# A two-block model step on one core: three weight pieces taken together at the start of each stage, their halves made ahead of the norm

## The reference

```python
mod = silu(c) @ w_ada + b_ada                 # shifts, scales, gates ("ada")
h = rms_norm(x, w) * (1 + sc1) + sh1
x = x + g1 * mixer(h)                         # gated delta rule; GLA; MLA
h = rms_norm(x, w) * (1 + sc2) + sh2
x = x + g2 * (silu(gu[:, :D_FF]) * gu[:, D_FF:]) @ w_out   # gu = h @ w_in
```

## Time and profile before

| | us |
|---|---|
| median of 3 runs | 1551.38 |
| lowest and highest | 1547.1, 1552.73 |
| profiled execution, its own time | 1547.16 |
| its span in the profile | 1545.6 |
| mean granted TensorE clock in it | 0.958 of 2.4 GHz |

### The profile page before, as it was taken

The page is one execution under the profiler, slowest core; times in us unless marked ns, Lnnn a source line. Parts: engine busy times, 40 slices in busy tenths (PEclk is TensorE's granted clock), DMA queues, the critical chain, the costliest instruction groups (busy, mean ns, idle before and its releaser), DMA issues.

```text
span 1545.6 us, 27829 instructions
## 1 busy us (share of the span) xinstructions
PE 1433.0 (93%) x10169; PEld 1261.8 (82%) x10169; DVE 747.8 (48%) x1452; ACT 644.4 (42%) x1171; POOL 14.8 (1%) x81
## 2 busy tenths in 40 slices
PE   5999999999998889999979998899998899899997
PEld 2977888887885678899947777799997678799997
DVE  0666656666532144455456543655553122555553
ACT  3454544445322044445364432555542222555542
POOL 3000000000000000000000000000000000000000
PEclk9899999999998989999979999899999889899999
DMA  8666457564553759965639983466564125266562
GB/s 292 178 206 203 150 151 232 187 196 136 166 148 125 214 151 290 273 183 160 173 109 291 282 271 96 137 185 181 162 180 157 29 86 135 70 185 180 167 187 83
DMA packets 400010, 269.89 MB, mean 175 GB/s; under 512 B 9914, under 2 KB 357424, under 8 KB 399936
## 3 DMA queue, kind: packets, MB, share of 16 engines
q1 hardware_dynamic: 399936, 268.83, 58.6%
HBM read 267.75 MB, written 1.05 MB: 174 GB/s over the span
## 4 chain that ended last, share of the span: by engine, by line
PE 76%; DMA 8%; DVE 7%; ACT 4%; issue 2%; SPq 2%; DVEq 0%; ACTq 0%
PE bank L715 16%; PE bank L716 15%; PE bank L717 15%; PE bank L680 5%; DMA w_raw<-in_w_in 4%; PE bank L758 4%; PE bank L651 3%; PE bank L666 2%; PE bank L1080 1%; DMA big<-in_w_ada 1%; DMA ring<-in_w_gdn_proj 1%; PE bank L888 1%; DVE w_low L1658 1%; PE bank L889 1%; PE bank L1112 1%
## 5 line engine op out<-in xcount | busy, mean ns | idle before, releaser
L715 PE MATMUL bank<-h_parts,w_high 128*128 128x256 f32 x1824 | 550.5, 302 | 17.0 <-DVE h_parts L1674 15.4
L716 PE MATMUL bank<-h_parts,w_high 128*128 128x256 f32 x1824 | 523.1, 287 | 0.0
L717 PE MATMUL bank<-h_parts,w_low 128*128 128x256 f32 x1824 | 522.4, 286 | 0.0
L1658 DVE TENSOR_TENSOR w_low<-w_raw,w_high 128x1024 fp32r<-128x1024 f32 (+2 forms) x324 | 359.5, 1122 | 184.2 <-ACT w_high L1223 184.0
L715 PEld LDWEIGHTS bank<-h_parts,w_high 128*128 128x128 f32 x1824 | 355.7, 195 | 43.8 <-issue 25.3
L716 PEld LDWEIGHTS bank<-h_parts,w_high 128*128 128x128 f32 x1824 | 357.5, 196 | 3.9 <-issue 3.6
L717 PEld LDWEIGHTS bank<-h_parts,w_low 128*128 128x128 f32 x1824 | 356.7, 196 | 0.0
L1223 ACT ACTIVATE w_high<-w_raw 128x1024 fp32r<-128x1024 f32 (+2 forms) x324 | 312.6, 973 | 81.4 <-DMA w_raw<-in_w_in 38.0
L1215 ACT ACTIVATE evac<-bank 128x256 f32<-128x256 f32 x140 | 53.9, 385 | 232.9 <-PE bank L717 183.3
L715 PE MATMUL bank<-act_parts,w_high 128*128 128x256 f32 x528 | 149.3, 283 | 0.0
L717 PE MATMUL bank<-act_parts,w_low 128*128 128x256 f32 x528 | 148.6, 281 | 0.0
(11 more groups left out here) (338 smaller groups left out, 1495.6 us busy)
## 6 DMA issues: line engine op xcount, KB each, us to landing
w_raw<-in_ffn_w_in SPq DMA_DIRECT2D x88, 512.0 KB, 3.8
w_raw<-in_w_in SPq DMA_DIRECT2D x72, 512.0 KB, 4.0
ada_w<-in_ada_w SPq DMA_DIRECT2D x34, 1024.0 KB, 5.4
w_raw<-in_w_ffn_in SPq DMA_DIRECT2D x44, 512.0 KB, 6.4
ada_w<-in_w_ada SPq DMA_DIRECT2D x16, 1024.0 KB, 11.5
w_raw<-in_gla_w_in SPq DMA_DIRECT2D x24, 512.0 KB, 6.4
w_raw<-in_ffn_w_out SPq DMA_DIRECT2D x32, 384.0 KB, 3.8
w_raw<-in_ffn_w_out SPq DMA_DIRECT2D x32, 320.0 KB, 3.0
```

What stands on the lines that cost most here:

```text
L715: pe.matmul(acc[:, 0:T], hi[:, n, :], x_parts[:, k, 0, :], start=k == 0, stop=False)
L716: pe.matmul(acc[:, 0:T], hi[:, n, :], x_parts[:, k, 1, :], start=False, stop=False)
L717: mm = pe.matmul(acc[:, 0:T], lo[:, n, :], x_parts[:, k, 0, :], start=False, stop=k == kb - 1)
L1658: dve.tensor_tensor(w_low[:, s, 0:m], w_raw[:, s, 0:m], w_high[:, s, 0:m].bitcast(F32), ALU.subtract)\
```

## The change

At each opening TensorE takes three pieces (two in the first mixer) together, one block of h after the other: for each block, nine (six) matmuls into three (two) banks. The high and low halves of those pieces are made ahead of the norm: in FFN 1 between the copies of w_o's product, in FFN 2 in the GLA's last head, in FFN 3 before the last heads' attention. The high half of the fourth piece comes directly behind the norm. `high` waits on another condition for first slots. The first round of hidden pieces uses four banks. `st_o2` and `st_o3` move to ring slots that leave `w_raw`, `w_high` and `w_low` free for pieces 0 to 2. In the first mixer the low halves of pieces 0 and 1 move ahead of the norm's scale. Between FFN 1 and the GLA the squares of the second norm go from ScalarE to VectorE, and GLA pieces 1 and 2 get their low halves before the next scaling; two `rows2` steps move. Nothing of SP's code is changed.

```diff
@@ SplitStream
+        self.parts_free = [max(Stream.slot_user.get(self.SLOTS + s, 0), Stream.slot_user.get(2 * self.SLOTS + s, 0)) for s in range(slots)]
@@ program
-        st_o2 = Stream(1, KB, [3, 7, 11, 16, 17, 0, 1, 2])
+        st_o2 = Stream(1, KB, [3, 7, 11, 16, 17, 12, 13, 14])
-        st_o3 = Stream(1, KB, SplitStream.SLOTS)
+        st_o3 = Stream(1, KB, [12, 13, 14, 15, 16, 17, 7, 11])
@@ TensorE, ffn
-                for i in range(6 if ada else 0):
+                pe.wait_ge(S("evacuated"), st_f.block0 + 3)
+                for k in range(KB):
+                    for j in range(3):
+                        split_product(st_f, 0, j, bank[j], h_parts, IN_PARTS[0], KB, ready=("h_low", parts_made) if j == 0 else None, part=[k])
+                split_product(st_f, 0, 3, bank[3], h_parts, IN_PARTS[0], KB)
+                for i in range(1, 6 if ada else 1):
                     hidden(i)
@@ TensorE, head1
-                    some(3 * KB)
+                    for k in range(KB):
+                        for j in range(2):
+                            split_product(st_h1, i, j, bank[j], h1_parts, IN_PARTS[0], KB, part=[k], ready=None if j else ("h_low", 0))
+                    at[0] = 2 * KB
+                    some(KB)
@@ TensorE, head2
-                    products(KB)
+                    for k in range(KB):
+                        for j in range(3):
+                            split_product(st_h2, i, j, bank[j], h1_parts, IN_PARTS[0], KB, part=[k], ready=None if j else ("h_low", LOW_OF[3] * KB))
+                    at[0] = 3 * KB
+                    rows2(2)
                     low_rank()
                     products(KB)
+                    rows2(3)
                     gate_channels()
-                    for step in range(2, 6):
+                    for step in range(4, 6):
@@ ScalarE, high
-                if st is not st_h1 or not (isinstance(i, int) and i == 0 and j < st.slots):
+                if isinstance(i, int) and i == 0 and j < st.slots:
+                    if st in (st_f1, st_f2, st_f3):
+                        act.wait_ge(S("gemm_done"), st.parts_free[j])
+                    elif st is not st_h1:
+                        act.wait_ge(S("gemm_done"), st.block0)
+                else:
                     act.wait_ge(S("gemm_done"), st.done(i, j) - st.slots)
@@ ScalarE, out_blocks
-                        copy_out(st, i, j, evac[:, j, :], 2, scale=mod[:, bass.ds(per * i + gate * KB + j, 1)])
+                        copy_out(st, i, j, evac[:, j, :], 2, scale=mod[:, c:c + 1])
+                        if (per * i + j) % 2 and per * i + j < 6:
+                            high(st_f, 0, (per * i + j) // 2, IN_PARTS)
@@ ScalarE, ffn
-                act.wait_ge(S("gemm_done"), st_f.block0)
-                high(st_f, 0, 0, IN_PARTS)
                 norm(n)
+                high(st_f, 0, 3, IN_PARTS)
                 for f in range(KB):
...
-                    if f % 4 == 3:
-                        high(st_f, 0, f // 4 + 1, IN_PARTS)
@@ ScalarE, between the stages
-            for f in range(KB):
-                act.wait_ge(S("h_ready"), 2 * KB + f + 1)
-                act.activation(sq[:, f, :], xT[:, f, :], ACT.Square).then_inc(S("norm_sq"), 1)
@@ ScalarE, the GLA's last head (behind its second token copy); and behind the MLA's last softmax, for st_f3
+                    for j in range(3):
+                        high(st_f2, 0, j, IN_PARTS)
@@ VectorE, add_blocks
+                        if f % 2 and f < 6:
+                            low(st_f, 0, f // 2, IN_PARTS)
@@ VectorE, ffn
-                low(st_f, 0, 0, IN_PARTS)
...
-                for j in (1, 2):
-                    low(st_f, 0, j, IN_PARTS)
@@ VectorE, between the stages
-            norm_apply(2, xT)
+            for f in range(KB + 1):
+                if f < KB:
+                    dve.scalar_tensor_tensor(xT[:, f, :], xT[:, f, :], nscale[:, f:f + 1], rstd[:, :], ALU.mult, ALU.mult).then_inc(S("h_scaled"), 1)
+                if f:
+                    dve.wait_ge(S("h_ready"), 2 * KB + f)
+                    dve.tensor_tensor(sq[:, f - 1, :], xT[:, f - 1, :], xT[:, f - 1, :], ALU.mult).then_inc(S("norm_sq"), 1)
+            for j in (1, 2):
+                low(st_h2, 0, j, IN_PARTS)
@@ VectorE, the GLA's last head; and behind the MLA's last softmax, for st_f3
+                    for j in range(3):
+                        low(st_f2, 0, j, IN_PARTS)
                     ada_bias(3, 0, 12, len(early) + H1 + st_pa.n + 12)
```

More of the change, by code:

```diff
@@ L731, in hidden @@
                             ada(i, j // 2)
-                for i in range(6 if ada else 0):
+                pe.wait_ge(S("evacuated"), st_f.block0 + 3)
[4 more added lines that the diff above has]
+                for i in range(1, 6 if ada else 1):
                     hidden(i)
-                with pe.Fori(6 if ada else 0, st_f.n) as i:
+                with pe.Fori(6 if ada else 1, st_f.n) as i:
                     hidden(i)
@@ L1421, in hidden @@
                         act.wait_ge(S("ffn_free"), first + 2 * i + j // 2 + 1)
-                        copy_out(st_f, i, j, evac[:, j, :], 2, func=ACT.Silu if j % 2 == 0 else ACT.Copy)
+                        copy_out(st_f, i, j, evac[:, j, :], 4 if isinstance(i, int) and i == 0 else 2, func=ACT.Silu if j % 2 == 0 else ACT.Copy)
                         if j < 1:
-                            high(st_f, i, j + 3, IN_PARTS)
+                            if not (isinstance(i, int) and i == 0):
+                                high(st_f, i, j + 3, IN_PARTS)
                         elif not last:
@@ L1429, in hidden @@
                         if j % 2:
-                            dst = act_parts[:, 2 * i + j // 2, 0, :] if last else act_parts[:, bass.ds(2 * i + j // 2, 1), 0, :]
+                            dst = act_parts[:, 2 * i + j // 2, 0, :] if isinstance(i, int) else act_parts[:, bass.ds(2 * i + j // 2, 1), 0, :]
                             act.wait_ge(S("ffn_act"), first + 2 * i + j // 2 + 1)
                             act.activation(dst, evac[:, j - 1, :], ACT.Copy).then_inc(S("act_high"), 1)
-                with act.Fori(0, st_f.n - 1) as i:
+                hidden(0)
+                with act.Fori(1, st_f.n - 1) as i:
                     hidden(i)
@@ L1534, in head2 @@
                 copies(5)
+                if not gemm:
+                    for j in range(3):
+                        high(st_f2, 0, j, IN_PARTS)
                 act.wait_ge(S("o2_done"), n)
@@ L1627, in _ @@
             softmax(st_h3.n - 1)
+            for j in range(3):
+                high(st_f3, 0, j, IN_PARTS)
             attended(st_h3.n - 1)
@@ L1700, in _ @@
             h_low(0, KB - 1, h1_parts)
-            for j in (1, 2):
-                low(st_h1, 0, j, IN_PARTS)
+            low(st_h1, 0, 2, IN_PARTS)
             dve.wait_ge(S("rows_landed"), 16 * n_table_dmas)
@@ L2006, in ffn @@
                 add_down(st_d, 2 + FFN_OF[n] * KB, batch)
-            add_blocks(st_o1, 4, "o_added", 4)
+            add_blocks(st_o1, 4, "o_added", 4, st_f1)
             def bias_ffn1():
@@ L2023, in _ @@
             h_low(3, KB - 1, h1_parts)
-            for j in (1, 2, 3):
-                low(st_h2, 0, j, IN_PARTS)
+            low(st_h2, 0, 3, IN_PARTS)
             dve.memset(segment, 1.0).then_inc(S("segment"), 1)
@@ L2183, in _ @@
             softmax(st_h3.n - 1)
+            for j in range(3):
+                low(st_f3, 0, j, IN_PARTS)
             add_pairs(st_o3, 4 + 2 * KB)
```

23 lines of the change are left out of this document (12 added, 11 removed).

## The result

The changed kernel takes 1558.39 us (median; 1553.85 to 1562.59) where the kernel before takes 1546.51 us in the same comparison: ratio 1.0074, 95% interval 1.0051 to 1.0098, 11.9 us slower. The profiled execution took 1561.79 us, its span is 1560.3 us and its mean granted clock 0.953, against 1545.6 us and 0.958 before.

The account below looks back on a forecast made before the run. TensorE, three quarters of the chain that ended last, was taken as the bound, mostly its split products. Lost 19.3 us less gained 7.8 made 11.5 us slower; 1551.4 + 11.5 is 1563 us, range 1553 to 1573.

Parts of the forecast that it names:

- The output projection: w_o before FFN 1: ScalarE waits for a piece's landing, TensorE stalls 7.4 us, slow clock 1.5 more; 8.9 us lost.
- From hidden to output: Each FFN: w_out's first high half waits for all hidden products, 2.3 us late; 6.9 us lost, plus 2.2 for clock.
- The last head: GLA's last head: FFN 2's low halves take 3.5 us on VectorE, 2.2 of it idle; 1.3 us lost.
- The FFN openings: First 72 products, interleaved with early halves: gains of 2.0 us in FFN 1, 1.4 in FFN 2, 2.3 in FFN 3.
- The bounds of 3 and 12 us: FFN and first mixer openings together: gain 3 us with 7 us at low clock, 12 with none; 6.8 taken.
- The first mixer's opening: First mixer's first 72 products, two pieces interleaved: 11.3 against 12.4 us, 1.1 us gained.
- The GLA: GLA stage, norms and interleaved opening up to piece 5: 1 us gained, between -1.5 and +2.5.
- the first (cheap waits): Rival for all gaps and openings: waits cost no clock, openings gain 2 us more; 1557 us, chance 0.24.
- The second: Rival in the first mixer's head loop: shifted transfers save 5 us on each of six, 1533 us; chance 0.04.
- The third: Rival at the openings: bank switching every third product keeps TensorE at 1.2 GHz, 24 us more, 1587 us; chance 0.05.

Follow-up runs that it names:

- e6: Changed kernel, but SP issues FFN 1's first three pieces behind the first four blocks of w_o instead of all eight: 1550.61 us, 1.0042 of the kernel before.
- e2: Changed kernel with FFN 1's three early high and low halves made behind the copies of w_o's blocks 5 and 6: 1550.25 us, 1.0018 of the kernel before.
- e1: Changed kernel with the old first-slot wait for all streams but those of the hidden pieces: 1554.31 us, 1.0041 of the kernel before.
- e5: Kernel before with only the wait of the w_out streams' first slots for all hidden products added: 1558.24 us, 1.0090 of the kernel before.
- e4: e3 with FFN 2's three low halves moved behind the state updates of the GLA's last head: 1539.98 us, 0.9945 of the kernel before.
- e9: e8 with the high half of each FFN's fourth piece made ahead of the norm: 1536.81 us, 0.9945 of the kernel before.
- e8: e4 with two instead of three pieces interleaved in the GLA's opening, gate channels one piece earlier: 1537.23 us, 0.9956 of the kernel before.
- e10: The same program as e4, run once more: 1539.70 us, 0.9961 of the kernel before.
- e7: e4, but TensorE takes the FFNs' first three pieces one after another: 1542.16 us, 0.9983 of the kernel before.
- e3: Changed kernel with the edits of e1 and e2 together: 1545.61 us, 0.9983 of the kernel before.
- e11: The same program as e8, run once more beside e10: 1537.01 us, 0.9950 of the kernel before.

## Why the prediction held

1563 us was forecast, 1558.4 measured (11.5 slower forecast, 11.9 measured). The mechanism was the one forecast: two added waits that cost more than the openings gain. That the difference was met to 0.4 us is luck in part: the terms below were off by up to 3 us each, and the errors cancel. The 4.6 us by which the time itself was missed come from the base: 1551.4 was the median of three executions, and that of eight is 1546.5.

- **The output projection** (7.4 us stall, 1.5 clock): 7.66 and 3.1. e6 shows the landing as the cause, e2 that the whole goes away with it. The clock term was too small, as I let only 16 products run slowly and the trace shows 3.1 us over 48; for those 16 my own rows gave 1.7 (5.22 less 3.5), not 1.5.
- **From hidden to output** (2.3 us three times, 0.7 each for the clock): 1.98 to 1.99, and no clock loss in the changed kernel. e1 shows the wait as the cause. With the clock neither end was wrong: e5 lost it behind two gaps of three.
- **The last head** (1.3): 1.1 by the gap, and 1.7 of clock that was not in the sum. e4 takes both away. I had charged a gap that grows only with its growth; behind the longer gap the products ran slowly too (5.41 us instead of 3.72). The other 1.6 us there are clock behind a gap that the change did not touch.
- **The FFN openings** (2.0, 1.4, 2.3): 2.7, 2.6, 3.8 over the first 72 products, 2.6, 2.5, 3.7 over the hidden stage. The 4 us at the low clock were about right (0.77 of 10.96 us is 5.0 us at half clock, 0.83 of 10.22 is 3.5); but at full clock a block's nine products took 1.08 us, not 1.2: the product with the wait was followed after 0.12 us like any other, where I had 0.25. The bounds of 3 and 12 us were not worked out well either: with my own costs, 7 us at the low clock give 2 and none 13. The fourth piece's high half cost 0.2 us (e9) where I had 0.4.
- **The first mixer's opening** (1.1): 1.6 us over the 72 products. By the end of the head loop the changed kernel is 4.4 us ahead, but that can't be put down to the change. The 32 small products of the gates behind the opening went from 5.18 to 3.75 us:

```profile
51.46 5.18 PE L801 MATMUL bank<-wab,hT 128*128 128x16 f32 x32
```

```profile
49.41 3.75 PE L807 MATMUL bank<-wab,hT 128*128 128x16 f32 x32
```

But e5, with the old opening, has 3.75 us too, and ends the loop 3.7 us ahead of the kernel before. The eleven traces with the new opening end it between 418.9 and 421.0 us, on both sides of e5's 419.8. So the opening gains 1.6 us, and no gain at the end of the loop is shown.

- **The GLA** (1.0): 0.9, from the norms. e8 shows that the later gate channels ate the rest.
- Two stretches are not explained by the change: +3.8 us before w_o and +3.1 in the MLA stage. Both vary between executions of the same code. From the head loop to w_o one program took 105.2 us in e4 and 107.8 in e10; its longest gap for a transfer was 3.4 us and 4.8 (2.8 before, 4.8 after). The MLA stage took 152.8 us before and 154.9 in e5, with one code, 155.4 in e4 and 152.5 in e7, with the other. TensorE's gaps in it sum to 22.4 us with the old code and 22.6 with the new, so it is the granted clock that differs (0.89 before, 0.88 in e5 and e4, 0.90 in e7). Ten of the eleven traces with the changed MLA code lie at 155.0 to 155.9, so a small cost of the halves made there, which I had put at nothing, is not excluded.
- Without these two stretches and the first mixer's the traces give 12.0 us, against 11.9 between the medians. That is as near as traces can tell, as the first mixer's 1.6 us are left out too, and 1.6 us of clock in the last head are in it.

Of the rivals, the first (cheap waits) was right about the clock at the three gaps, and that the openings gain more (10.8 us over their first 72 products, where I had 6.8). It was wrong at w_o, where the clock cost 3.1 us, and its 5.6 us slower are half of what was measured. The second asked for 3.3 us a head in the head loop; the loop gave 0.9 us in all behind its start. The third, bank switching that keeps TensorE at the lower of its levels, is refuted: in the openings banks switch at every third product and the granted clock rose, to 0.77 to 0.83. The Trainium skill's account of cycling through banks (TensorE: Matmul & The Clock Gate, section A second HAM failure mode: psum-queue depth-cycling) rests on short idle times between groups of matmuls. It does not carry over to this case, where TensorE had no idle time between the banks.

## What to carry to other kernels

When the condition of a wait is rewritten for one case, list every stream that now takes the new branch: here a cautious default for first slots also took in the output pieces and cost a 2 us gap at three places. Work made early on an in-order engine must have its data landed when its turn comes, or everything queued behind it waits for the transfer; ask where SP issues that transfer. And early work belongs behind the instruction that another engine waits for, in front of the engine's idle time, not ahead of it. And before a difference between two traces is put down to a change, look for another trace with the old code in that stage: e5 showed 3.7 of the 4.4 us in the first mixer without the change.

## What the runs showed of the hardware

**A gap of 2 to 3 us is a draw on the clock.** Gaps of 1.98 to 1.99 us before the output pieces kept the full clock nine times of nine in the changed kernel, e2 and e6, and lost it twice of three in e5. The 2.65 us gap of the earlier trace rows, which every kernel here has, was followed by 16 products in 3.72 us in six of the thirteen traces (before and e4 among them) and in 5.28 us or more in seven (after and e3 among them). At one place it was no draw: behind the state product a gap of 2.30 or 2.31 us was followed by 16 products in 5.41 us in all five kernels that have it (after, e1, e2, e3, e6), and one of 1.18 us by 3.72 us in the eight others. A loss is 1.5 to 2.1 us in most cases and 3.0 once (e11, 16 products in 6.69 us), so a short gap can cost its length and about as much again.

**The spread between executions goes with the granted clock.** The eight executions of the changed kernel, in us, with their mean clock: 1553.85 (0.962), 1553.87 (0.960), 1556.41 (0.959), 1558.12 (0.958), 1558.66 (0.958), 1558.73 (0.957), 1561.79 (0.953), 1562.59 (0.952). Time and clock have a correlation of -0.96. 8.7 us, more than most of the terms here, separate executions of one program, so a single profiled execution can't place a difference of a few microseconds. Its stretches can, but not all of them: from the last head to FFN 2's first product one program took 55.8 us in e8 and 60.2 in e11, with the same gaps and another clock behind two of them.
